# Mixer of a hybrid encoder layer: finest level without decays, far blocks and chunk ends on the ScalarE, some decays in PSUM, a different order of side work

## Time and profile before

| | us |
|---|---|
| median of 3 runs | 1093.55 (1093.36 to 1095.13) |
| the profiled execution's own time | 1093.68 |
| its span | 1091.3 |
| PE busy in the span | 1053.1 (96%) |
| DVE busy | 584.4 (54%) |
| ACT busy | 407.6 (37%) |
| POOL busy | 152.5 (14%) |

### The profile page before, as it was taken

The page is one execution under the profiler, slowest core; times in us unless marked ns, Lnnn a source line. Parts: engine busy times, 40 slices in busy tenths (PEclk is TensorE's granted clock), DMA queues, the critical chain, the costliest instruction groups (busy, mean ns, idle before and its releaser), DMA issues.

```text
span 1091.3 us, 13753 instructions
## 1 busy us (share of the span) xinstructions
PE 1053.1 (96%) x4920; PEld 862.0 (79%) x4920; DVE 584.4 (54%) x748; ACT 407.6 (37%) x521; POOL 152.5 (14%) x144
## 2 busy tenths in 40 slices
PE   8999999999999999989998889999999999999997
PEld 6778888888888887767786667878888888888886
DVE  4467777733423256489798997463333333322323
ACT  5242222222312134665774664343222222221211
POOL 0111111100001010145444352200000000000100
PEclk9999999999999999999999999999999999999999
DMA  9668888622322242111121111212222222222222
GB/s 359 244 198 284 293 285 293 225 96 96 97 96 97 96 143 97 66 70 59 39 78 39 58 40 59 78 58 97 96 96 96 96 96 96 96 97 96 97 96 77
DMA packets 37568, 132.93 MB, mean 122 GB/s; under 512 B 4128, under 2 KB 4384, under 8 KB 37408
## 3 DMA queue, kind: packets, MB, share of 16 engines
q1 hardware_dynamic: 29024, 100.83, 27.1%
q0 software_dynamic: 8512, 31.66, 8.7%
HBM read 130.37 MB, written 2.10 MB: 121 GB/s over the span
## 4 chain that ended last, share of the span: by engine, by line
PE 86%; DVE 9%; issue 3%; ACT 2%; DMA 0%; DVEq 0%; SPq 0%; ACTq 0%
PE psum L1235 25%; PE psum L1237 25%; PE psum L1236 25%; PE psum L1523 2%; PE psum L1338 2%; PE psum L1493 1%; DVE qk L1084 1%; DVE wlo L738 1%; DVE qk L1083 1%; PE psum L1537 1%; PE psum L1373 1%; PE psum L1331 1%; PE psum L1464 1%; PE psum L1466 1%; PE psum L1465 1%
## 5 line engine op out<-in xcount | busy, mean ns | idle before, releaser
L738 DVE TENSOR_TENSOR wlo<-raw,whi 128x1024 fp32r<-128x1024 f32 x166 | 209.3, 1261 | 323.7 <-ACT whi L377 322.5
L377 ACT ACTIVATE whi<-raw 128x1024 fp32r<-128x1024 f32 x164 | 173.6, 1059 | 530.8 <-PE psum L1237 523.0
L1235 PE MATMUL psum<-hhi,whi 128*128 128x512 f32 x896 | 357.4, 399 | 8.3 <-DVE sg L1035 5.4
L1237 PE MATMUL psum<-hhi,wlo 128*128 128x512 f32 x896 | 351.1, 392 | 0.0
L1236 PE MATMUL psum<-hlo,whi 128*128 128x512 f32 x896 | 350.8, 392 | 0.0
L1235 PEld LDWEIGHTS psum<-hhi,whi 128*128 128x128 f32 x896 | 169.7, 189 | 49.4 <-DVE wlo L738 7.9
L1236 PEld LDWEIGHTS psum<-hlo,whi 128*128 128x128 f32 x896 | 169.8, 190 | 35.5 <-issue 1.4
L1237 PEld LDWEIGHTS psum<-hhi,wlo 128*128 128x128 f32 x896 | 169.3, 189 | 35.9
L1235 PE MATMUL psum<-ghi,whi 128*128 (+1 forms) x352 | 137.2, 390 | 0.0
L1237 PE MATMUL psum<-ghi,wlo 128*128 (+1 forms) x352 | 137.0, 389 | 0.0
L1236 PE MATMUL psum<-glo,whi 128*128 (+1 forms) x352 | 136.9, 389 | 0.0
(11 more groups left out here) (186 smaller groups left out, 938.0 us busy)
## 6 DMA issues: line engine op xcount, KB each, us to landing
raw<-wu SPq DMA_DIRECT2D x168, 512.0 KB, 3.3
ada<-wada POOLq DMA_DIRECT2D x56, 512.0 KB, 4.9
early<-wada SPq DMA_DIRECT2D x16, 512.0 KB, 15.2
x<-xt SPq DMA_DIRECT2D x4, 512.0 KB, 5.1
out<-outt SPq DMA_DIRECT2D x8, 256.0 KB, 2.2
bd<-bd POOLq DMA_DIRECT2D x1, 1024.0 KB, 5.2
csr<-c_rows POOLq DMA_DIRECT2D x1, 512.0 KB, 5.3
dif<-consts POOLq DMA_DIRECT2D x1, 448.0 KB, 6.2
```

Of the source, the lines that this page charges most:

```text
L377: nc.scalar.activation(whi[:, slot, :], raw[:, slot, :], ACT.Copy).then_inc(hi_done, 1)
L738: nc.vector.tensor_tensor(wlo[:, slot, :], raw[:, slot, :], whi[:, slot, :], ALU.subtract).then_inc(lo_done, 1)
L1235: nc.tensor.matmul(dst, a, rhi, start=start, stop=False)
L1237: return nc.tensor.matmul(dst, b, rhi, start=False, stop=stop)
```

## The change

1. Level 1 (e = 8, step 9) takes no exponential. In it one token decays into its neighbour by f = 1 - k, which is already there. DVE writes the even columns of both operands as `(k_odd - 1) * even`, with two instructions over 256 columns; ACT writes the odd columns as negated copies, after step 7 has been scored (`odd_done`). POOL's two differences and the exponential of that level go.
2. Decay 1 (chunk ends): ACT computes `exp(tot - cum)` itself, in 8 pieces of 128 columns with `tot` as the bias. POOL's L346 goes.
3. `decay_far` moves from DVE to ACT: 4 pieces of 128 columns, behind `decay(r, 2)`.
4. In heads 1 and 2 the decays with odd e (1, 3, 5, 7) are written to PSUM banks 2 and 3.
5. Other places. `recur` is split into `recur_input` (two instructions) and the scan. Of the forward pass, pieces 2 and 3 move into head 0 (inputs gaps 2 and 3, scans gaps 5 and 7). Backward pieces: inputs 0 and 1 in gap 1 of head 1, scans in gaps 5 and 6; piece 2 in gap 0 of head 2; piece 3 in gaps 3 and 7. `one_minus_a2`, `gate_sums`, `gate_post`, `rg_exp`, `rg_root`, `gelu`, `z_post`, `logs`, `o_copy`, `o_sums`, `o_root`, `o_rb` and `o_norm` move by some gaps.

```diff
+        Z_ACT_AT = ((2, 3, 5, 6, 9), (1, 2, 5, 7, 8), (0, 3, 5, 6, 9))
+        Z_DVE_AT = ((2, 3, 5, 8, 10), (2, 4, 6, 8, 10), (1, 4, 6, 9, 10))
+        def decays(h, e):
+            return psum[:, 2:4, :] if 0 < h < 3 and e % 2 else dec[:, e % 2]
...
@@ gpsimd
-                nc.gpsimd.tensor_tensor(dif[:, 1]..., tot[:]..., cum[:, p]..., ALU.subtract).then_inc(dif_done, 1)
-                for i, hw in enumerate(LEVELS):
+                for i, hw in enumerate(LEVELS[:-1]):
...
@@ scalar, decay(h, e)
+                elif e == 8:
+                    act.wait_ge(scored, STEPS * h + 8)
+                    nc.scalar.activation(qk[:, 0, :, 1:T:2], w3[:, h % 2, 1:3, 1:T:2], ACT.Copy, scale=-1.0).then_inc(odd_done, 1)
+                elif e == 1:
+                    for lane in range(2):
+                        for c in range(TC):
+                            ins = nc.scalar.activation(decays(h, 1)[:, lane, c * P:(c + 1) * P], cum[:, h % 2, lane, c * P:(c + 1) * P],
+                                                       ACT.Exp, bias=tot[:, lane, c:c + 1], scale=-1.0)
+                    ins.then_inc(dec_done, 1)
+            def decay_far(h):
+                act.wait_ge(qk_done, 10 * h + 2)
+                act.wait_ge(etot_done, h + 1)
...
+                    ins = nc.scalar.activation(far[:, i, :], qk[:, e, lane, c * P:(c + 1) * P], ACT.Copy,
+                                               scale=etot[:, h % 2, lane, by:by + 1])
...
@@ scalar, order
                 if r == 3:
                     gelu(2)
                     gelu(3)
+                decay(r, 2)
+                decay_far(r)
...
-                    if r and g == 0:
+                    if (r, g) in ((1, 0), (2, 0), (3, 2)):
                         o_copy(r - 1)
-                    if r == 1 and g == 4:
+                    if (r, g) == (1, 0):
                         rg_root(1)
-                        if g % 2:
-                            z_post(first + g // 2)
+                    for k in range(5):
+                        if r < 3 and g == Z_ACT_AT[r][k]:
+                            z_post(first + k)
+                    if r < 3 and g == (5, 6, 5)[r]:
+                        logs(r + 1)
...
@@ vector, decayed(h, e)
+                elif e == 8:
+                    kf, q_, kb = (w3[:, p, i, :] for i in range(3))
+                    nc.vector.scalar_tensor_tensor(qk[:, 0, 1, 0:T:2], kf[:, 1:T:2], 1.0, kf[:, 0:T:2], ALU.subtract, ALU.mult)
+                    nc.vector.scalar_tensor_tensor(qk[:, 0, 0, 0:T:2], kb[:, 0:T:2], 1.0, q_[:, 0:T:2], ALU.subtract,
+                                                   ALU.mult).then_inc(qk_done, 1)
@@ vector, order
+            recur_input(0, 0)
             recur(0, 0)
+            recur_input(0, 1)
             recur(0, 1)
             z_post(10)
             sum_logs(0)
-            recur(0, 2)
             z_post(11)
             far_scores(0)
-            recur(0, 3)
...
-                    if 0 < r < 3 and g == 7:
+                    if (r, g) == (1, 9):
                         o_norm(r - 1)
+                    if (r, g) == (3, 0):
+                        o_norm(1)
-                    if r == 2 and g in (2, 4):
-                        recur(1, 1 + g // 2)
-                        y_rg(g // 2 - 1)
+                    if (r, g) == (2, 0):
+                        recur_input(1, 2)
+                    if (r, g) == (2, 0):
+                        recur(1, 2)
...
@@ tensor
+                    if e == 8:
+                        pe.wait_ge(odd_done, h + 1)
-                    if r and g == (1 if r == 3 else 3):
+                    if (r, g) in ((1, 3), (2, 2), (3, 2)):
                         o_sums(r - 1)
-                    if 0 < r < 3 and g == 6:
+                    if (r, g) in ((1, 9), (2, 9)):
                         o_rb(r - 1)
```

More of the change, by code:

```diff
@@ L362, in _ @@
                 if h == 0:
+                    square_a(1, 1)
                     square_a(1, 2)
@@ L675, in _ @@
                     y_upper(1)
-                decay(r, 2)
                 if r == 3:
@@ L689, in _ @@
                         nc.scalar.preload_act_table(ACT.Sqrt)
-                    if r and g == (5 if r == 3 else 4):
+                    if (r, g) in ((1, 4), (2, 4), (3, 3)):
                         o_root(r - 1)
-                    if r == 1 and g == 4:
+                    if (r, g) == (1, 0):
                         rg_root(1)
-                    if r == 2 and g == 1:
+                    if (r, g) == (2, 2):
                         gelu(0)
                         gelu(1)
[L697 to L700, removed]
-                        if g % 2:
-                            z_post(first + g // 2)
[L703 to L707, removed]
+                    if r < 3 and g == (9, 8, 9)[r]:
+                        decay(r + 1, 0)
+                    if r < 3 and g == (9, 8, 9)[r]:
+                        decay(r + 1, 1)
+                    for k in range(5):
[3 more added lines that the diff above has]
+                        logs(r + 1)
+                    if (r, g) == (0, 3):
+                        gate_post(1, 0)
+                    if (r, g) == (0, 4):
+                        rg_exp(1, 0)
+                    if (r, g) == (0, 3):
+                        gate_post(1, 1)
+                    if (r, g) == (0, 4):
+                        rg_exp(1, 1)
+                    if (r, g) == (0, 7):
+                        gate_post(1, 2)
+                    if (r, g) == (0, 7):
+                        rg_exp(1, 2)
+                    if (r, g) == (0, 7):
+                        gate_post(1, 3)
+                    if (r, g) == (0, 8):
+                        rg_exp(1, 3)
                     if r == 3:
@@ L1076, in decayed @@
                         dve.wait_ge(zq_done, QG_COUNT[("q", h)])
-                    nc.vector.tensor_tensor(qk[:, e], dec[:, e], w3[:, p, 1 - e:3 - e, :], ALU.mult).then_inc(qk_done, 1)
-                elif e < 9:
+                    nc.vector.tensor_tensor(qk[:, e], decays(h, e), w3[:, p, 1 - e:3 - e, :], ALU.mult).then_inc(qk_done, 1)
+                elif e < 8:
                     hw = LEVELS[e - 2]
                     q5 = qk[:, e % 2].rearrange("p l (n two w) -> p l n two w", two=2, w=hw)
-                    d5 = dec[:, e % 2].rearrange("p l (n two w) -> p l n two w", two=2, w=hw)
+                    d5 = decays(h, e).rearrange("p l (n two w) -> p l n two w", two=2, w=hw)
                     w5 = w3[:, p].rearrange("p l (n two w) -> p l n two w", two=2, w=hw)
@@ L1172, in _ @@
                             mask_in_block(r, s - 1)
-                    if r < 3 and g and g % 2 == 0:
-                        z_post(first + g // 2 - 1)
+                    for k in range(5):
+                        if r < 3 and g == Z_DVE_AT[r][k]:
+                            z_post(first + k)
+                    if r < 3 and g == 7:
+                        sum_logs(r + 1)
                     if r == 3 and g in (3, 5):
                         lo_u(U_OUT + g // 2 + 1)
-                    if r < 3 and g == 7:
-                        sum_logs(r + 1)
@@ L1180, in _ @@
-                    if r and g == (6 if r == 3 else 5):
+                    if (r, g) in ((1, 6), (2, 6), (3, 5)):
                         rms_inverse(r - 1, orms_done, orinv_done)
-                    if 0 < r < 3 and g == 7:
+                    if (r, g) == (1, 9):
                         o_norm(r - 1)
[L1184 to L1187, removed]
-                    if r == 2 and g in (2, 4):
-                        recur(1, 1 + g // 2)
-                        y_rg(g // 2 - 1)
+                    if (r, g) == (3, 0):
+                        o_norm(1)
@@ new lines, in _ @@
+                    if (r, g) == (0, 2):
+                        recur_input(0, 2)
+                    if (r, g) == (0, 5):
+                        recur(0, 2)
+                    if (r, g) == (0, 3):
+                        recur_input(0, 3)
+                    if (r, g) == (0, 7):
+                        recur(0, 3)
+                    if (r, g) == (1, 1):
+                        recur_input(1, 0)
+                    if (r, g) == (1, 5):
+                        recur(1, 0)
+                    if (r, g) == (1, 1):
+                        recur_input(1, 1)
@@ new lines, in _ @@
+                    if (r, g) == (1, 6):
+                        recur(1, 1)
+                    if (r, g) == (2, 0):
+                        recur_input(1, 2)
+                    if (r, g) == (2, 0):
+                        recur(1, 2)
+                    if (r, g) == (2, 3):
+                        recur_input(1, 3)
+                    if (r, g) == (2, 7):
+                        recur(1, 3)
+                    if (r, g) == (0, 8):
+                        one_minus_a2(1, 0)
+                    if (r, g) == (2, 2):
+                        y_rg(0)
@@ L1191, in _ @@
+                    if (r, g) == (0, 8):
```

(26 more changed lines are left out.)

48 lines of the change are left out of this document (20 added, 28 removed).

## The result

The changed kernel takes 1069.65 us (median of 4, 1067.49 to 1071.53) against 1093.45: a ratio of 0.9778, 95% interval 0.9757 to 0.9799. The forecast was 1073.5 with a range of 1066 to 1085. Its profiled execution took 1069.36 us with a span of 1067.7, 23.6 less than before.

The account below looks back on a forecast made before the run. PE idles waiting for DVE, itself the bound in heads 1 and 2. Of 30.1 us winnable, 7.0 left at places and 3.0 for order leave a gain of 20.1: 1073.5 us, range 1066 to 1085.

Parts of the forecast that it names:

- What could be won: Four head windows: PE's 23.4 us idle plus 6.7 us of half clock, at most 30.1 us to win.
- Ahead of head 0: PE's 5.41 us wait for `z_post(11)` and 3.6 us of half clock go; 0.3 and a new 1.2 us remain.
- Decay 1: Head 0, step 0: eight ACT pieces take 1.9 us against 1.06 before, giving PE a new 1.2 us wait.
- Odd decays in PSUM: Heads 1 and 2: four of six products per head escape 0.86 us each beside POOL, 3.4 us per head.
- Level 1: Each head: two DVE instructions of 256 columns at 0.35 us instead of two of 512 at 0.60, gain 0.5 us.
- Ends of heads 1 and 2: `o_norm(0)` between head 1's last masks makes PE 0.5 us late; mask and weight subtraction make `pv(2)` 1.0 late.
- Step 4's 0.4: Head 1: `rg_root` in gap 0 delays ACT's decay 3; step 4 can bear it to within 0.4 us.
- Order losses in heads 0 to 2: DVE with 2 us to spare per head loses 1.0 us each to strict order, 3.0 together.
- Head 3: ACT's far blocks come 1.6 us late and PE stands 2.0 us before `o_sums`; DVE waits not added.
- PE as the bound in all four heads: DVE's work falls 7.8 us in heads 1 and 2, 4.4 less in 0 and 3, below PE's own in all four.
- DVE stays the bound: Rival, 22%: only the two large stalls go, 1082 us; 1080 if PSUM products aren't immune.
- ACT parks: Mechanism of rival "slower", 8%: `z_post` in five places one gap before PE is done holds ACT up to 3.63 us each; 1100.

Follow-up runs that it names:

- e7: Kernel before with only forward recurrences 2 and 3 moved behind the unit and the products that head 0 waits for: 1094.51 us, ratio 1.0002.
- e9: Kernel before with only forward recurrences 2 and 3 moved behind the unit, the products and the next unit as well: 1097.34 us, ratio 1.0027.
- e3: Changed kernel with all decays in SBUF, none in PSUM: 1071.08 us, ratio 0.9787.
- e6: Changed kernel with level 1 by decays again: 1079.87 us, ratio 0.9872.
- e10: Changed kernel with level 1 by decays again and the next head's logs in gap 6 of every head: 1082.58 us, ratio 0.9888.
- e2: Kernel before, in its old order, with the changed kernel's arithmetic (items 1 to 4): 1086.5 us, ratio 0.9940.
- e1: Changed kernel's order with the arithmetic of the kernel before (items 1 to 4 undone): 1093.13 us, ratio 0.9994.
- e5: Changed kernel with decay 1 made as before, difference by POOL and one exponential: 1069.58 us, ratio 0.9774.
- e12: Changed kernel with head 3 reordered: decay 2 and far blocks before gelu, output copy in gap 1, norm and lower y moved: 1066.99 us, ratio 0.9747.

## Why the prediction was right

- **What could be won.** 30.1 us of idle time and half clock in the mixer; 22.6 were won there. Forecast 20.1.
- **Ahead of head 0.** Left over 0.3 + 1.2; measured 0 + 0.92, no half clock. Right, though with the whole change only: e7 and e9 show that the two later places tried for the whole recurrence pay nothing. I had argued the removal without pricing that; the sums per head happened to cover it.
- **Decay 1.** Eight pieces at 1.9 from rows; they take 2.45 us. One piece of 128 columns lasts 0.39 us into SBUF and 0.35 into PSUM, so my slope between 256 and 512 columns was the mis-sized step. The estimate of 2.35 from "VectorE: DVE Perf Modes" of the Trainium skill, The TRN2 errata, was the better one.
- **Odd decays in PSUM.** Four of six products per head stand beside POOL (numbers 3 and 5) and none is slowed, as forecast. The size was too large: in e3, with these decays in SBUF, the six products take 2.7 us more in head 1 and 1.9 in head 2, where 3.4 each were forecast, since not every one is caught for a full 0.86. The rule of "SBUF — State Buffer" of the Trainium skill, Who interferes with whom, holds for a product with one PSUM operand. The section makes an exception that the prediction left out, for instructions that read their one SBUF input through both of DVE's ports; L1093, which reads one SBUF tensor, took 0.28 to 1.15 us. What the PSUM decays are worth to the time I had let come through whole; e3 finds 1.4 us of 6.8, with part of the loss hidden by head 3.
- **Level 1.** Sized at 0.5 + 1.3 us of DVE per head with POOL's share; the two short instructions take 0.42 us each, not 0.35. Undone it costs 10.2 us. This is the term I got most wrong: I counted the instructions saved, and e6's rows show DVE waiting for the exponential in ACT's queue. How much of the 10 us is that wait and how much the added work, e10 leaves open.
- **Ends of heads 1 and 2.** 0.5 and 1.0 forecast, 0.31 and 0.43 us before `pv` measured. Step 4's 0.4: nothing.
- **Order losses in heads 0 to 2.** 3.0 forecast, none measured. That is most of the difference between 1073.5 and 1069.65.
- **Head 3.** `far` 1.6 forecast, 2.05 measured; `o_sums` 2.0 against 0.84; and a wait of 1.10 for product 3 with half clock (1.8) that I had ruled out. 3.6 forecast, 5.8 measured with the clock.
- **PE as the bound in all four heads.** Right in heads 0 to 2 (PE busy 130.3 of 132 us). DVE's busy time fell by 32.7 us where 2 x 7.8 + 2 x 4.4 = 24.4 were forecast; the arithmetic alone (e2) takes off 20, and the rest comes with the order. The rival "DVE stays the bound" is out. "ACT parks" didn't reach PE in the changed kernel (ACT stood at most 3.25 us before a conversion in heads 0 to 2, and no wait of PE follows); e10 has it at 4.10 us, with PE's 5.47 us behind.

The main mechanism is shown: with both halves of the change PE waits 1.7 us for DVE up to the end of head 2, with either half alone it waits over 10. That the number came within 4 us is in part luck, since errors of both signs met: 0.6 us too much left over for head 0 and 4.2 for the ends, step 4 and the order, 2.2 too little for head 3 and its clock. That makes 7.5 us left over where 10.0 were forecast. The profiled execution's gain is 24.3 us: 24.0 in the mixer's windows, less 0.4 outside them, and 0.7 between the span and the device time, for which I have no cause.

## What to carry to other kernels

When several engines walk a hand-written order, price a removed instruction by the queue it stood in and by who waits behind it; here level 1 by decays cost 10 us in the new order though it adds only a few us per head to DVE and POOL. A block of side work that delays the bound engine may have to be cut and spread: moved as a whole it only moved the wait (e7, e9), and cut into inputs and scans over four gaps it left no wait in the changed kernel and one of 0.64 us in e1. Test the new order without the lighter work and the lighter work without the new order: here they gave nothing and 0.6% alone, 2.2% together. And when a part that is undone costs nothing, look for a later wait that hides the loss (e5 and head 3).

## What the runs showed of the hardware

- A DVE product of 512 columns with one operand in PSUM keeps 0.68 to 0.69 us beside a POOL instruction; with both in SBUF it took 1.51 and 1.65 at the same place (e3), and 0.93 to 1.76 at others.
- ACT writes 1024 columns of exponentials into PSUM in 1.03 us, into SBUF in 1.05 to 1.06, and 128 columns with a bias in 0.35 and 0.39: hardly a gain.
- In the profiled execution of the changed kernel PE waited 2.05 us up to 619.5, 1.10 up to 629.0 and 0.84 up to 631.0. The granted clock was 1.00 until 632 and about 0.5 from there to 635, and a matmul of 512 columns took 0.63 us in place of 0.39:

```profile
630.00:635.00 5.00, 4.16 (x18) 3.34 (x17) 4.71 (x5) 4.78 (x7) 2.88 (x3) 0.71 0.00 0
```

In e12, with waits of 0.87, 1.26 and 0.62 us, the clock stayed at 1.00 in the same stretch. Whether the waits made the difference isn't shown: the mean clock of the changed kernel itself was between 0.993 and 0.999 in its four executions.
